# Joined repairs in the down projections, the loads of value pages and the layer loop, and level scores for the later queries alone

## The reference

```
for l in range(2):
    h = h + 0.5 * swiglu1(rmsnorm(h))             # hidden width 2816
    z = rmsnorm(h) @ w_in                          # one projection for all mixers and gates
    branches = [conv(z), retention(z), gated_linear_attention(z), differential_attention(z)]
    h = h + (sum_i sigmoid(gate_i) * (branch_i @ w_b_i)) @ w_out
    h = h + 0.5 * swiglu2(rmsnorm(h))

swiglu(x) = (silu(x @ wg) * (x @ wu)) @ wd
```

## Time and profile before

| | before |
|---|---|
| median of 3 runs | 2910.8 us (2909.86 to 2912.94) |
| profiled execution, its own time | 2914.48 us |
| its span | 2912.9 us |
| granted TensorE clock, mean of the span | 0.993 |
| PE busy | 2866.3 us (98%) |
| DVE busy | 2040.4 us (70%) |
| ACT busy | 1230.1 us (42%) |
| POOL busy | 121.1 us (4%) |

### The profile page before, as it was taken

One profiled execution on the slowest core, in us unless ns is written; L12 is line 12 of the kernel. 1 busy time (PEld: TensorE's weight loads), 2 busy tenths in 40 slices (PEclk: granted clock), 3 DMA queues, 4 the chain that ended last, 5 costly groups with the idle time before them and its releaser, 6 DMA issues.

```text
span 2912.9 us, 59977 instructions
## 1 busy us (share of the span) xinstructions
PE 2866.3 (98%) x21668; PEld 2743.9 (94%) x21668; DVE 2040.4 (70%) x3643; ACT 1230.1 (42%) x2192; POOL 121.1 (4%) x219
## 2 busy tenths in 40 slices
PE   8999999999999999999999999999999999999998
PEld 7999999988889999999999999998878899999998
DVE  8889434567657688886488893346666576888854
ACT  6446223435325254454254452243352343544632
POOL 0000001220000000000000000012100000000000
PEclk9999999999999999999999999999999999999999
DMA  4223225562324312223222222436423243122232
GB/s 143 91 86 105 99 82 181 172 198 77 109 70 157 137 61 88 99 87 112 77 74 87 101 103 93 138 126 206 159 72 109 86 161 121 61 101 86 101 102 91
DMA packets 102131, 321.00 MB, mean 110 GB/s; under 512 B 13503, under 2 KB 30063, under 8 KB 100272
## 3 DMA queue, kind: packets, MB, share of 16 engines
q1 hardware_dynamic: 89424, 277.03, 27.3%
q0 software_dynamic: 12512, 41.43, 4.4%
HBM read 290.62 MB, written 29.12 MB: 110 GB/s over the span
## 4 chain that ended last, share of the span: by engine, by line
PE 90%; DVE 4%; issue 3%; POOLq 1%; ACT 1%; DMA 0%; POOL 0%; DVEq 0%; SPq 0%; ACTq 0%
PE ps L1304 46%; PE ps L1333 34%; PE ps L1483 3%; PE ps L1316 2%; PE ps L1749 1%; PE ps L1545 1%; POOLq L615 1%; DVE Z L2321 1%; DVE w_lo L1875 1%; PE ps L1621 0%; POOL vpage L616 0%; PE ps L1595 0%; PE ps L1771 0%; PE ps L1645 0%; PE ps L1644 0%
## 5 line engine op out<-in xcount | busy, mean ns | idle before, releaser
L1875 DVE TENSOR_TENSOR w_lo<-w_raw,w_hi 128x1024 fp32r<-128x1024 f32 x240 | 292.5, 1223 | 369.1 <-ACT w_hi L727 366.1
L1333 PE MATMUL ps<-x_more,w_hi 128*128 128x296 f32 x2112 | 460.3, 299 | 2.1 <-DVE p_copy L2028 1.4
L1333 PE MATMUL ps<-x_hi,w_hi 128*128 128x296 f32 x1408 | 421.6, 299 | 3.4 <-DVE hT L2146 2.1
L1333 PE MATMUL ps<-x_hi,w_lo 128*128 128x296 f32 x1408 | 422.2, 300 | 0.0
L1333 PE MATMUL ps<-x_lo,w_hi 128*128 128x296 f32 x1408 | 422.1, 300 | 0.0
L727 ACT ACTIVATE w_hi<-w_raw 128x1024 fp32r<-128x1024 f32 x224 | 234.7, 1053 | 396.7 <-PE ps L1304 198.8
L1304 PE MATMUL ps<-x_hi,w_hi 128*128 128x296 f32 x1600 | 371.7, 314 | 1.8 <-ACT hT L1054 1.6
L1913 DVE TENSOR_TENSOR w_lo<-w_raw,w_hi 128x512 fp32r<-128x512 f32 x444 | 299.5, 689 | 96.6 <-ACT w_hi L775 96.3
L1333 PEld LDWEIGHTS ps<-x_more,w_hi 128*128 128x128 f32 x2112 | 351.2, 188 | 4.3 <-DVE p_copy L2028 2.4
L1304 PE MATMUL ps<-x_lo,w_hi 128*128 128x296 f32 x1600 | 350.3, 300 | 0.0
L1304 PE MATMUL ps<-x_hi,w_lo 128*128 128x296 f32 x1600 | 349.8, 300 | 0.0
(11 more groups left out here) (367 smaller groups left out, 5089.5 us busy)
## 6 DMA issues: line engine op xcount, KB each, us to landing
w_raw<-wstream SPq DMA_DIRECT2D x420, 512.0 KB, 3.5
kpage<-cache_k SPq DMA_DIRECT2D x128, 128.0 KB, 2.9
vpage<-cache_v POOLq DMA_DIRECT2D x128, 128.0 KB, 3.2
gate_rows<-hT SPq DMA_DIRECT2D x48, 296.0 KB, 2.5
d_sg<-gate_rows SPq DMA_DIRECT2D x16, 888.0 KB, 4.7
h_rows<-hT SPq DMA_DIRECT2D x2, 1480.0 KB, 6.2
hT<-h_rows SPq DMA_DIRECT2D x2, 1480.0 KB, 6.3
hT<-h_in SPq DMA_DIRECT2D x4, 592.0 KB, 8.1
```

The lines of the kernel that those rows point to most:

```text
L1333: mm = pe.matmul(ps[:, bank, 0:HALF], wp[:, k, :], xp, start=new and k == 0 and n == 0, stop=k == KH - 1 and n == 2, skip_group_check=True)
L1875: v.tensor_tensor(w_lo[:, slot, :, :], w_raw[:, slot, :, :], w_hi[:, slot, :, :].bitcast(F32), ALU.subtract).then_inc(weights_low, 1)
```

## The change

Four parts.

**Down projection and joins.** PE's `residual` becomes `down`, which walks `DOWN_ORDER`: output tile 1's first unit comes right behind output tile 0's first unit, and the pairs of banks are taken in another order. The units of tile 1 wait for `pair_steps` (a count of DVE's and ACT's steps on the last hidden tile). The first two waits of `ffn` for `residual_added` change places. DVE makes the first hidden tile's low part one step earlier, and the last steps of `ffn` on DVE and ACT come in another order.

**Value pages.** POOL reads the 16 page numbers of a pair ahead of the wait for `sample_pv`, and issues the 16 transfers behind it.

**Layers.** `Fori(0, DEPTH)` on all five engines becomes a Python loop, so the code of both layers stands one behind the other.

**Level scores.** Above level 0 only the later halves' queries are kept, packed in `g_ql`, and move through PE: 64 columns in place of 128 (in the first window 8 in place of 80 for blocks of 16, and 40 in place of 80 for blocks of 8, 4 and 2). The stationary keys stay 128 (80) columns. DVE copies as many fewer elements.

The diff, cut to its core:

```
-OUT_PAIRS = (1, 0, 2, 3)
+OUT_PAIRS = (1, 2, 0, 3)
+DOWN_ORDER = ((0, 0), (1, 0), (0, 1), (0, 2), (1, 1), (1, 2)) + tuple((j, u) for j in (2, 3) for u in range(3))
...
+def later_queries(n, w):
+
+    c0, cols = window(w)
+    b = LEVELS[n - 1]
+    first = max(c0, level_start(b))
+    return first, (c0 + cols - first) // b, (first - level_start(b)) // 2
...
-            def load_values(l, p):
-
-                for b in (2 * p, 2 * p + 1):
-                    for pg in range(PAGES):
-                        page = pl.value_load(pages[0:1, b * PAGES + pg:b * PAGES + pg + 1], min_val=0, max_val=POOL - 1)
-                        pl.dma_start(vpage[:, b % 2, pg, :], cache_v[ds(l * POOL + page, 1)].rearrange("a p n -> (a p) n")).then_inc(values_loaded[b % 2], 16)
+            def page_numbers(p):
+
+                return [pl.value_load(pages[0:1, n:n + 1], min_val=0, max_val=POOL - 1) for n in range(2 * p * PAGES, 2 * (p + 1) * PAGES)]
+
+            def load_values(l, numbers):
+
+                for n, page in enumerate(numbers):
+                    b2, pg = divmod(n, PAGES)
+                    pl.dma_start(vpage[:, b2, pg, :], cache_v[ds(l * POOL + page, 1)].rearrange("a p n -> (a p) n")).then_inc(values_loaded[b2], 16)
...
+                numbers = page_numbers(1)
                 pl.wait_ge(sample_pv, 1)
-                load_values(l, 1)
+                load_values(l, numbers)
...
+                    numbers = page_numbers(p)
                     pl.wait_ge(sample_pv, p)
-                    load_values(l, p)
+                    load_values(l, numbers)
...
-                tanh(N0 + KF - 1)
                 hidden_tiles(6, 8)
                 act.wait_ge(products_done, last + 7)
-                hidden_tiles(8, 12)
                 out_unit(3)
-                hidden_tiles(12, KF)
+                hidden_tiles(8, 10)
+                tanh(N0 + KF - 1)
+                hidden_tiles(10, KF)
...
-                        pe.wait_ge(residual_added, l * 24 + 8 + 11 if f else l * 24 + 3)
+                        pe.wait_ge(residual_added, l * 24 + 8 + 10 if f else l * 24 + 2)
...
-                pe.wait_ge(residual_added, l * 24 + 8 + 10 if f else l * 24 + 2)
+                pe.wait_ge(residual_added, l * 24 + 8 + 11 if f else l * 24 + 3)
...
+                    for j, u in DOWN_ORDER:
+                        pos = j * 3 + u
+                        unit_ready(l * QUADS + first // RING + i * 3 + pos // RING, pos % RING)
+                        if u == 0:
+                            pe.wait_ge(residual_added, l * 24 + r0 + i * 4 + j + 1)
+                        if (j, u) == (1, 0):
+                            pe.wait_ge(pair_steps, PAIR_STEPS * (hidden + KF - 1 + 2) + 3)
+                        elif (j, u) == (2, 0):
+                            pe.wait_ge(pair_steps, PAIR_STEPS * (hidden + KF - 1 + 2) + 6)
+                        bank, count = OUT_PAIRS[j], DOWN_BLOCKS[u]
+                        if j == 0:
+                            for k in range(count):
+                                pe.wait_ge(hidden_ready, hidden + 8 * u + k + 1)
+                                last = products(bank, pos % RING, (k, k + 1), 8 * u + k, hid_hi, hid_lo, start=u == 0 and k == 0,
+                                                stop=u == 2 and k == count - 1)
+                        else:
+                            last = products(bank, pos % RING, (0, count), 8 * u, hid_hi, hid_lo, start=u == 0, stop=u == 2)
+                        if (j, u) == (0, 2):
+                            last.then_inc(units_multiplied, 2)
+                        elif (j, u) != (1, 0):
+                            last.then_inc(units_multiplied, 1)
...
+                            mm = pe.matmul(ps[0:cols, h, 0:cols], k[:, c0:c0 + cols], q[:, c0:c0 + cols], start=True, stop=True)
                         else:
-                            k, q = g_kl[32 * h:32 * h + 32, n % 2, :], g_ql[32 * h:32 * h + 32, n % 2, :]
-                        mm = pe.matmul(ps[0:cols, h, 0:cols], k[:, c0:c0 + cols], q[:, c0:c0 + cols], start=True, stop=True)
+                            first, blocks, at = later_queries(n, w)
+                            count = blocks * LEVELS[n - 1] // 2
+                            mm = pe.matmul(ps[0:cols, h, 0:count], g_kl[32 * h:32 * h + 32, n % 2, c0:c0 + cols],
+                                           g_ql[32 * h:32 * h + 32, n % 2, at:at + count], start=True, stop=True)
...
-            with pe.Fori(0, DEPTH) as l:
+            for l in range(DEPTH):
+                gate_blocks[0] = 0
                 ffn(l, 0, U_FFN1)
-                residual(l, 0, U_DOWN1, DOWN_BLOCKS, hid_hi, hid_lo, l * 2 * KF)
+                down(l, 0, U_DOWN1, l * 2 * KF)
...
+                    if kind == "one to go":
+                        hidden_low(0, 1)
...
-                pair_(N0 + KF - 2, quad0 + KF // 2 - 1, 0, KF - 2, "steady")
+                pair_(N0 + KF - 2, quad0 + KF // 2 - 1, 0, KF - 2, "one to go")
 
                 N = N0 + KF - 1
                 v.wait_ge(weight_steps, W_STEPS * (N + 1))
                 v.sem_inc(weights_low, 2 * KF)
-                hidden_low(0, 1)
                 split_low(quad0 + KF // 2, 0)
                 quarter(N, 0, tmp[:, 0, HALF:T], BANK_E, a_copy)
-                hidden_low(1, 2)
                 quarter(N, 1, c22, 1, e_copy)
-                hidden_low(2, 3)
+                hidden_low(1, 3)
                 quarter(N, 2, tmp[:, 0, 0:HALF], BANK_B, first_copy[1])
+                hidden_low(3, 6)
+                split_low(quad0 + KF // 2, 1)
+                hidden_low(6, 8)
+                split_low(quad0 + KF // 2, 2)
+                split_low(quad0 + KF // 2, 3)
                 gate_ready(N, 1)
-                split_low(quad0 + KF // 2, 1)
+                hidden_low(8, 10)
                 hidden_tile(N, 1, KF - 1, 7)
-                hidden_low(3, 10)
-                split_low(quad0 + KF // 2, 2)
                 hidden_low(10, KF)
-                split_low(quad0 + KF // 2, 3)
...
+                        first, blocks, _ = later_queries(n, w)
+                        size = LEVELS[n - 1]
+                        c = first - window(w)[0]
+
+                        def later(ap):
+                            return ap[:, :, c:cols].rearrange("p h (n b) -> p h n b", b=size)[:, :, :, size // 2:size]
+
+                        v.copy_predicated(later(dst), later(mask).bitcast(U32).to_broadcast([cols, H, blocks, size // 2]),
+                                          ps[0:cols, 0:4, 0:blocks * size // 2].rearrange("p h (n b) -> p h n b", b=size // 2)
+                                          ).then_inc(lvl_taken, 1)
...
-                    return half((g_ql if part else g_kl)[:, (n + 1) % 2, :]), half(Z[:, GQ if part else GK, :]), half(g_e[:, n % 2, :])
+                    if part:
+                        room = g_ql[:, (n + 1) % 2, 0:(T - c0) // 2].rearrange("p (n b) -> p n b", b=size // 2)
+                    else:
+                        room = half(g_kl[:, (n + 1) % 2, :])
+                    return room, half(Z[:, GQ if part else GK, :]), half(g_e[:, n % 2, :])
```

38 lines of the change are left out of this document (11 added, 27 removed).

## The result

The changed kernel takes 2886.46 us in the median of 5 runs (2884.82 to 2889.35) beside 2909.86 (5 runs, 2905.67 to 2912.94) for the kernel before: a ratio of 0.992 with a 95% interval of 0.9908 to 0.9931, or 23.4 us. The forecast was 2888, and its range held.

A forecast was written before the change was run, and what follows sets the result against it. PE, busy for 98% of the span, was taken to bound the kernel. Gains of 7.1 + 3.5 + 8.7 + 3.6 = 22.9 us, scaled to the median of 2910.8, gave 2888 us; own range 2883 to 2892, 8-in-10 range 2880 to 2897.

The forecast's parts named there:

- Joins, forecast 7.1 us: Four joins into the down projection: PE's two stalls and the slow matmuls behind them go, 1.77 us a join; bounds 0 and 7.1.
- margin of 0.3 us for ring slot 3: At a join, DVE ends its work by 286.1 us and PE's second unit is due at 286.4.
- R3: Rival, joins: the wait only moves, ring slot 3's low part late by 1 to 1.8 us each; 2892 to 2895, chance 0.09.
- the last tile's repair: Joins, on DVE: it comes some 7 us later but hides, as PE has two more units, 13 us, to do first.
- Loop, forecast 3.5 us: Between the layers: without the branch, PE's 2.38 us gap and the half clock behind it go; bounds 2 and 5.5.
- The term for the clock: Behind the gap between layers, 15 matmuls at half clock cost 1.4 us, gone with the gap if it goes.
- Value pages, forecast 8.7 us: Pair 2's values in both layers: PE's waits for the last page and the slow matmuls behind them go; bounds 0 and 8.7.
- R1: Rival, value pages: they stay late, as the busy DMA engines move them no sooner; 0 to 3 us gained, 2895, chance 0.15.
- Level scores, forecast 3.6 us: Level items: 64 fewer streamed columns save 0.059 us an item over 56 items, plus 0.36 for the first window; bounds 0 and 9.
- what it left for a loaded column: Level items: a column both loaded and streamed costs 0.0025 us, of which 0.00093 was given to the stream.
- The two rows: Level items of four heads in PE's chain: 0.43 us with 128 columns and 0.31 us with 80.
- R4: Rival, level items: PE's clock falls among them as less is streamed, 23 us a layer, 2934 in all; chance 0.02.

The follow-up runs named there:

- one variant: The changed kernel with whole windows of queries in the level scores again, on PE and in DVE's copies: 2890.33 us, ratio 0.993 to the kernel before.
- the second set: The changed kernel run again without an edit: 2886.40 us (4 runs), ratio 0.9911 to the kernel before.

## Why the prediction was right

**Joins, forecast 7.1 us.** Both stalls went, at all four joins, 0.52 and 1.05 us each with the slow first matmul behind them; the part taken back cost 8.2. The margin of 0.3 us for ring slot 3, on which rival R3 stood, was 0.42. The step by which the last tile's repair "hides" held too, and the run with PE's old order shows what it hides behind: PE's extra unit of 6.5 us. The waits taken away are 5.5 us in that trace; the rest of the 8.2 is slower steps behind them and noise.

**Loop, forecast 3.5 us.** The gap of 2.38 us went, and PE's loop was all of it, not `hT`. With the measured steps in the prediction's own sum, 2.38 - 0.12 for the gap, 0.1 for the first matmul, 1.4 for the clock and 0.22 against it make 3.5 between the two profiles; taken back, the loop cost 3.0, with an interval of 4. The term for the clock, 1.4 of the 3.5, is the weak one: with all five loops back the gap came without it.

**Value pages, forecast 8.7 us.** The wait and the slow matmuls behind it went in both layers; taken back they cost 9.5. The way there was tighter than written, and that it still held is in part luck. The 16 reads for pair 2 took 8.7 us, not 7, so its first transfer came at 577.9, not 575.0, and its last at 588.1, not 587. A landing took 4.0 us in the median and not 3.2. And PE asked for the values at 592.61, not at 594.7: PE comes 2.1 us sooner, an estimated 1.8 of it (0.62 + 1.15) by the repaired first join, which the prediction left out of this part. With the median landing 588.1 + 4.0 = 592.1 leaves an estimated 0.5 us, where 1 to 4 us should have been, and in one variant the page was 0.74 us late. Of what the margin lost, PE's earlier question took the most (2.1), POOL 1.1 and the slower landing 0.8. R1 (the busy DMA) is this last one; it was real and did not decide.

**Level scores, forecast 3.6 us.** An item lost 1.460 - 1.397 = 0.063 us, where 0.059 was forecast; 56 of them, and the forecast's 0.36 for the first window's eight (six of them lost 0.033 us each, where 0.037 was forecast), make 3.9. That the part taken back cost 3.9 too says little, with an interval of 4 us. The price of a streamed column was right (0.0009 forecast, 0.0008 to 0.0010 measured); what it left for a loaded column (0.0025 - 0.0009 = 0.0016) was not, that is 0.0008. The two rows differ by 0.12 us for 48 columns of each kind, and these prices explain some 0.08 of it; the rest stays open. R4, the clock falling among the items, did not happen: 1.00 from 785 to 842 us.

**The sum.** Forecast 22.9 us, measured 23.4. So close a hit is luck: the ratio's interval allows 20 to 27 us, and the second set gave 26.1 beside its own runs of the kernel before. That the profiles differ by 28.0 is chance in the main: the profiled execution of the kernel before, 2914.48 us, lay 4.6 over this set's median, and had 6.8 us more at half clock outside the repaired places. The forecast summed only what the edits touch, and so had no term for such stretches.

## What to carry to other kernels

- When a view of waits names a tile that the waiting work doesn't need, look at the waiting engine's own queue: a taken branch of 3.8 us over a long loop body left a gap of 2.3 us on PE, which was put down to `hT`. Writing out the loop of two rounds removed it.
- Reads of addresses belong ahead of the wait that holds the transfers back. Gathered behind the wait they cost more (17 us lost) than in turn with the transfers (9.5).
- When several repairs go in together, redo each margin with the others' gains: here PE asked 2.1 us sooner for the pages, most of it by the repaired join.
- Where two engines share a repair, move both orders: the producer's new order alone was no better than the old pair.

## What the runs showed of the hardware

- In an item of four products of 32 rows in float32, a loaded and a streamed column cost about the same, 0.0008 to 0.0010 us for the four together.
- A load of 32 rows in float32 took 183 ns with 128 columns, 143 with 80 and 129 with 64.
- POOL issues 16 pages' transfers each 0.68 us (0.58 within a bunch) when the numbers are at hand, each 1.23 us when it reads each number first. The median landing was 3.2 us with reads and transfers in turn (two kernels), 3.8 and 4.0 in the two profiles of the changed kernel, and 4.4 where pair 2's start 8 us earlier.
- A gap of 2.3 us on PE was followed by a clock of 0.55 to 0.61 in two kernels and by 1.00 in a third. One kernel, run twice without an edit, showed its stretches at half clock in different places, 17.0 us in sum both times.
